# Operands of the up-projection made inside the out-projection, a reordered chain of head tiles, and the mixers' last stores moved behind their block

## The reference

```python
h = rms_norm(x, attn_norm_g); proj = h @ w_in            # 1024 -> 3600
q, k, v, z, xbc, dt_raw = split(proj)
attn_out = dilated_attention(q, k, v, q_norm_g, k_norm_g) # q and k normed per head; three patterns
ssm_out = ssd_mixer(z, xbc, dt_raw, ...)                  # conv, chunked scan, gate, rms_norm
x = x + concat(attn_out, ssm_out) @ w_out                 # 1536 -> 1024
x = x + conv_ffn(x, ffn_norm_g, w_up, ..., w_down)        # 1024 -> 5632, conv, gate, 2816 -> 1024
x = x + sigmoid(rms_norm(x, ple_norm_g) @ w_ple_gate) * (p @ w_ple_proj)
```

## Time and profile before

| What | us |
|---|---|
| Median of three runs | 3021.07 |
| Profiled execution | 3021.69 |
| Its span, first to last instruction | 3019.9 |
| PE busy | 2908.9 |
| DVE busy | 1999.8 |
| ACT busy | 1140.0 |
| POOL busy | 282.2 |

### The profile page before, as it was taken

How to read it: one execution, slowest core, us unless ns; L and a number is a source line. 1 busy time by engine, 2 the same in 40 slices (tenths; PEclk the granted TensorE clock), 3 DMA queues, 4 the chain that set the end, 5 groups by cost and what they waited for, 6 DMA issues and landing times. The chain is left out here.

```text
span 3019.9 us, 38703 instructions
## 1 busy us (share of the span) xinstructions
PE 2908.9 (96%) x14818; PEld 2296.6 (76%) x14818; DVE 1999.8 (66%) x2493; ACT 1140.0 (38%) x1735; POOL 282.2 (9%) x278
## 2 busy tenths in 40 slices
PE   8999999998989999899999999899999999999999
PEld 6788887875656566788778888788888788877887
DVE  7434555128566654545698899889998786776743
ACT  6321212112435353212254544544444444444321
POOL 0000000003433442000001000000000000000000
PEclk9999999998999999999999999999999999999999
DMA  4652222238585663643332244425543756453632
GB/s 150 201 164 75 63 82 68 63 112 202 169 213 146 193 173 103 205 143 115 141 110 79 98 147 156 179 90 192 193 153 105 257 200 227 146 158 114 195 115 67
DMA packets 260125, 435.04 MB, mean 144 GB/s; under 512 B 44049, under 2 KB 128529, under 8 KB 252913
## 3 DMA queue, kind: packets, MB, share of 16 engines
q1 hardware_dynamic: 255570, 408.32, 42.8%
q0 software_dynamic: 4384, 24.41, 2.3%
HBM read 312.18 MB, written 120.00 MB: 143 GB/s over the span
## 5 line engine op out<-in xcount | busy, mean ns | idle before, releaser
L103 PE MATMUL up_banks<-up_x_hi,up_w_hi 128*128 128x512 f32 x1232 | 483.5, 392 | 23.8 <-DVE up_x_lo L2734 8.2
L105 PE MATMUL up_banks<-up_x_hi,up_w_lo 128*128 128x512 f32 x1232 | 481.6, 391 | 0.0
L104 PE MATMUL up_banks<-up_x_lo,up_w_hi 128*128 128x512 f32 x1232 | 481.3, 391 | 0.0
L103 PE MATMUL inp_ps<-inp_h_hi,carry_q 128*128 128x512 f32 x896 | 352.9, 394 | 9.9 <-DVE inp_h_lo L200 9.8
L104 PE MATMUL inp_ps<-inp_h_lo,carry_q 128*128 128x512 f32 x896 | 349.7, 390 | 0.0
L105 PE MATMUL inp_ps<-inp_h_hi,carry_k_two 128*128 128x512 f32 x896 | 349.5, 390 | 0.0
L103 PEld LDWEIGHTS up_banks<-up_x_hi,up_w_hi 128*128 128x128 f32 x1232 | 232.4, 189 | 79.7 <-DVE up_w_lo L2667 16.1
L105 PEld LDWEIGHTS up_banks<-up_x_hi,up_w_lo 128*128 128x128 f32 x1232 | 232.3, 189 | 49.1
L104 PEld LDWEIGHTS up_banks<-up_x_lo,up_w_hi 128*128 128x128 f32 x1232 | 232.6, 189 | 47.8 <-issue 0.2
L2775 DVE SCALAR_TENSOR_TENSOR carry_rows<-carry_squares,up_conv_w,carry_rows 128x1024 f32<-128x1024 f32 x176 | 232.2, 1319 | 24.4 <-ACT carry_rows L2606 19.5
L103 PE MATMUL down_banks<-down_x_hi,down_w_hi 128*128 128x512 f32 x616 | 240.6, 391 | 7.1 <-DVE down_x_lo L2246 7.1
(11 more groups left out here) (384 smaller groups left out, 5332.6 us busy)
## 6 DMA issues: line engine op xcount, KB each, us to landing
carry_room<-in_w_up_dram SPq DMA_DIRECT2D x84, 512.0 KB, 4.4
act<-carry_rows SPq DMA_DIRECT2D x44, 512.0 KB, 2.8
carry_room<-cum_rows SPq DMA_DIRECT2D x16, 1024.0 KB, 6.8
carry_room<-x SPq DMA_DIRECT2D x7, 2048.0 KB, 9.8
carry_room<-in_w_in_dram SPq DMA_DIRECT2D x26, 512.0 KB, 6.0
xbc<-carry_room SPq DMA_DIRECT2D x12, 1024.0 KB, 5.7
carry_room<-xbc SPq DMA_DIRECT2D x16, 768.0 KB, 4.5
down_x<-act SPq DMA_DIRECT2D x12, 1024.0 KB, 7.4
```

Of the source, the lines that this page charges most:

```text
L103: pe.matmul(out, w_hi, x_hi, start=first, stop=False, skip_group_check=onto)
L104: pe.matmul(out, w_hi, x_lo, start=False, stop=False, skip_group_check=onto)
L105: return pe.matmul(out, w_lo, x_hi, start=False, stop=last, skip_group_check=onto)
```

## The change

Three parts.

1. **Head tiles.** DVE's split of the coming weights moves behind the low half of tile t-1, and ACT's high half of them behind the high half of t-1. SP's `spread_inverses` is cut in two: `fold_roots` now comes ahead of SP's wait for the split weights and the load of the next ones, the rest stays behind the load. `add_up(2)` in product 3 comes before k = 5 instead of k = 3, in products 4 and 5 before k = 4; from product 6 on it stays at 3.
2. **Mixers' end.** The last round's fold goes to a place of its own, and its inverse on DVE, its two stores and the store of `y_root` are issued by the out-projection's block: on SP ahead of `load(None)`, with the waits for all of them, on DVE ahead of k = 1.
3. **Up-projection's operands.** The high and low halves of A11, A12 and S1 and the difference S1 are made in the out-projection: 12 ACT and 16 DVE instructions, on DVE between the 16 of L1929 and `finish(NB - 1)`. The up-projection raises its semaphores by their counts instead.

```diff
-def column_tile(pe, out, w_hi, w_lo, h_hi, h_lo, mm_done, between=None):
+def column_tile(pe, out, w_hi, w_lo, h_hi, h_lo, mm_done, between=None, ahead=3):
-        if k == 3 and between:
+        if k == ahead and between:
...
-            def spread_inverses(t):
+            def fold_roots(t):
                 sp.wait_ge(ps_free, t + 1)
                 if t > 0:
                     sp.wait_ge(inverse_st, 16 * t)
                 for e in range(2):
                     sp.dma_start(fold[HD * e:HD * e + HD, :], roots[16 * e:P:32, :]).then_inc(folded, 16)
+
+            def spread_inverses(t):
                 sp.wait_ge(inv_done, t + 1)
...
                 else:
+                    if 2 <= t < QKT + 2:
+                        fold_roots(t - 2)
                     sp.wait_ge(wlo_done, t + 1)
                 sp.dma_start(w_raw[t % 2], w_tiles[(t + 2) * P:(t + 3) * P, :]).then_inc(w_in_s[t % 2], 16)
...
-                    split(t, 0, b) if t % 2 == 0 else split(t - 1, 0, b)      # ACT
                 if 0 < t <= QKT:
                     high(t - 1)
+                if t > 0:
+                    split(t, 0, b) if t % 2 == 0 else split(t - 1, 0, b)
...
                     evacuate(t, b, stage[b])                                  # DVE
-                    split(t - b, 0, b)
                 if 0 < t <= QKT:
...
                     low_part(t - 1)
+                if t > 0:
+                    split(t - b, 0, b)
...
-            product(3, 1, ps_free, lambda: add_up(2, 0))
+            product(3, 1, ps_free, lambda: add_up(2, 0), None, 5)
             for i in range(1, QKT // 2 - 1):
-                product(i * 2 + 2, 0, ps_free, lambda: add_up(i * 2 + 1, 1))
-                product(i * 2 + 3, 1, ps_free, lambda: add_up(i * 2 + 2, 0))
+                product(i * 2 + 2, 0, ps_free, lambda: add_up(i * 2 + 1, 1), None, 4)
+                product(i * 2 + 3, 1, ps_free, lambda: add_up(i * 2 + 2, 0), None, 4)
...
-            sp.dma_start(self.mix_t[r * P:(r + 1) * P, :], out).then_inc(self.o_st, 16)
+            if r < KVH - 1:
+                sp.dma_start(self.mix_t[r * P:(r + 1) * P, :], out).then_inc(self.o_st, 16)
...
+    def last_stores(self, sp):
+        sp.dma_start(self.mix_t[(KVH - 1) * P:KVH * P, :], self.out_last[:, :]).then_inc(self.o_st, 16)
+        self.store_inverse(sp, KVH - 1)
         sp.wait_ge(self.o_st, 16 * KVH)
         sp.wait_ge(self.inv_st, 16 * KVH)
...
+            mixer.store_root(sp)             # out_projection, SP
+            heads.last_stores(sp)
+            sp.wait_ge(mixer.root_st, 16)
             load(None)
...
+                    if first and k == 1:     # out_projection, DVE
+                        heads.invert(dve, KVH - 1)
...
+            for v, freed in ((A11, 2), (A12, 8), (S1, 4)):        # out_projection, ACT
+                act.wait_ge(k_done, NB * MIXT + freed)
+                for q in range(Q):
...
+                    act.activation(x_hi[:, v, q], at, ACT.Copy).then_inc(next_hi, 1)
...
+            dve.wait_ge(carry.normed, 2 * KD)                     # out_projection, DVE
+            dve.wait_ge(k_done, NB * MIXT + 4)
+            next_low(0, A11)
+            dve.wait_ge(k_done, NB * MIXT + 6)
+            for q in range(Q):
+                dve.tensor_tensor(x_raw[:, S1, q], carry.x_blk[1][:, q], carry.x_blk[0][:, q], ALU.subtract).then_inc(next_t1, 1)
+            dve.wait_ge(k_done, NB * MIXT + 10)
+            next_low(1, A12)
+            next_low(2, S1)
             finish(NB - 1)
...
             dve.wait_ge(carry.normed, 2 * KD)                     # up_projection, DVE
+            dve.sem_inc(x_lo_s, 3 * Q)
             weights(0)
-            tokens(0, 0)
             s1(0)
             weights(1)
-            tokens(0, 1)
-            for q in range(Q):
-                dve.tensor_tensor(x_raw[:, S1, q], x_blk[1][:, q], x_blk[0][:, q], ALU.subtract).then_inc(t1_s, 1)
             weights(2)
             s2(0)
-            tokens(0, 2)
```

More of the change, by code:

```diff
@@ L695, in turn, with product @@
                 last.then_inc(v_turned, 1)
-            def product(t, b, free, between=None, into=None):
+            def product(t, b, free, between=None, into=None, ahead=3):
                 pe.wait_ge(wlo_done, t + 1)
                 pe.wait_ge(free, t - 1)
-                column_tile(pe, ps[b] if into is None else ps[into], w_hi[:, b], w_lo[:, b], h_hi, h_lo, mm_done, between)
+                column_tile(pe, ps[b] if into is None else ps[into], w_hi[:, b], w_lo[:, b], h_hi, h_lo, mm_done, between, ahead)
             def time_steps():
@@ L1022, in sync_inverses, with store_inverse @@
     def sync_inverses(self, sp):
[L1023 removed]
+        for r in range(KVH - 1):
             yield self.at(2, r, 1.0) + self.OUT + 1.0
[L1025 to L1027 removed]
+            self.store_inverse(sp, r)
+    def store_inverse(self, sp, r):
+        sp.wait_ge(self.den_inv, r + 1)
+        sp.dma_start(self.den_rows[2 * r:2 * r + 2, :].rearrange("e (c s) -> (e c) s", s=32), self.fold(r)[:, 0, :]
+                     ).then_inc(self.inv_st, 16)
+    def last_stores(self, sp):
+        sp.dma_start(self.mix_t[(KVH - 1) * P:KVH * P, :], self.out_last[:, :]).then_inc(self.o_st, 16)
+        self.store_inverse(sp, KVH - 1)
         sp.wait_ge(self.o_st, 16 * KVH)
@@ L1178, in add, with fold, invert @@
             dve.tensor_tensor(den[0:2 * 32], bank[0:2 * 32, 1], den[0:2 * 32], ALU.add).then_inc(self.o_add, 1)
+    def fold(self, r):
+        return self.fold_last if r == KVH - 1 else self.den_fold
     def inverses(self, dve):
-        for r in range(KVH):
+        for r in range(KVH - 1):
             yield self.at(2, r, 1.0) + self.OUT
-            dve.wait_ge(self.den_in, 32 * (r + 1))
-            dve.tensor_tensor(self.den_fold[:, 0], self.den_fold[:, 0], self.den_fold[:, 1], ALU.add).then_inc(self.den_add, 1)
-            dve.wait_ge(self.den_add, r + 1)
-            dve.reciprocal(self.den_fold[:, 0], self.den_fold[:, 0]).then_inc(self.den_inv, 1)
+            self.invert(dve, r)
+    def invert(self, dve, r):
+        fold = self.fold(r)
+        dve.wait_ge(self.den_in, 32 * (r + 1))
+        dve.tensor_tensor(fold[:, 0], fold[:, 0], fold[:, 1], ALU.add).then_inc(self.den_add, 1)
+        dve.wait_ge(self.den_add, r + 1)
+        dve.reciprocal(fold[:, 0], fold[:, 0]).then_inc(self.den_inv, 1)
     def tensor(self, pe):
@@ L1770, in out_projection @@
     with Phase(nc, "outp") as ph:
+        Q = KD // 2
+        A11, S1, A12 = 0, 1, 3
+        with nc.sbuf_tensor("up_x_hi", [P, 7, Q, 512], F32R) as x_hi:
+            with nc.sbuf_tensor("up_x_raw", [P, 7, Q, 512], F32) as x_raw:
+                pass
+            with nc.sbuf_tensor("up_x_lo", [P, 7, Q, 512], F32R) as x_lo:
+                pass
+        carry.up_x = x_hi, x_raw, x_lo
         w_hi = ph.sb("w_hi", [P, MIXT, D], F32R)
@@ L2351, in up_projection @@
     with Phase(nc, "up") as ph:
-        x_hi = ph.sb("x_hi", [P, 7, Q, 512], F32R)
-        with nc.sbuf_tensor("up_x_raw", [P, 7, Q, 512], F32) as x_raw:
-            pass
-        x_lo = ph.sb("x_lo", [P, 7, Q, 512], F32R)
+        x_hi, x_raw, x_lo = carry.up_x
+        for part in ("hi", "lo"):
+            ph.sb(f"x_{part}_place", [P, 7, Q, 512])
         w_hi = ph.sb("w_hi", [P, RING, 512], F32R)
@@ L2614, in take_root @@
                 act.activation(rstd[n], banks[:, 3 if n == 2 else 7], ACT.Sqrt, bias=carry.eps[:, 0:1], scale=1.0 / D).then_inc(rooted, 1)
-            for n in range(3):
-                weights(n)
-                tokens(0, n)
-            for s in range(3, RING):
+            act.sem_inc(x_hi_s, 3 * Q)
+            for s in range(RING):
                 weights(s)
```

43 lines of the change are left out of this document (26 added, 17 removed).

## The result

The changed kernel takes 3008.9 us (median of 7 runs, 3006.48 to 3014.09), the kernel before 3025.6 us (median of 7, 3020.65 to 3029.64). The ratio is 0.9949, with a 95% interval of 0.9938 to 0.9960: faster by 0.4 to 0.6%, which is 12 to 19 us. The profiled pair differs by 15.2 us (3021.69 and 3006.48 us), where the prediction's sum was 15.0.

A forecast was written before the change was run, and what follows sets the result against it. The prediction took PE, busy 96% of the span, to bound the kernel. Its terms 3.1 + 6.5 + 5.4 = 15.0 us came off 3021.69 to give 3006.7, stated as 3006 us; range for 8 in 10, 3000 to 3013.

The forecast's parts named there:

- three terms: Whole kernel: gains of 3.1 us at the head tiles, 6.5 at the mixers' end and 5.4 at the up-projection.
- Head tiles, 3.1 us forecast: Head tiles: the chain decides add_up(5), 169.9 against 173.46, 3.6 us gained, less 0.5 for lost clock.
- N + 17.55: Head tiles: tile t+2's evacuation comes 17.55 us after N(t), the start of multiplying by tile t's inverse roots; unchanged.
- N(3): Head tiles: start of the multiplication by tile 3's inverse roots, put at 148.1 with 22.5 us per tile.
- N(0): Head tiles: start of the multiplication by tile 0's inverse roots, at 80.59, claimed to stay.
- its own refutation: Head tiles: the forecast is wrong if norm_rows lands more than 4.5 us after its issue.
- the rival with the load ahead of the roots: Head tiles: norm_rows waits behind SP's weight load, N(t+1) 2.4 us later per tile, 3013 us in all; chance 0.25.
- 3.4 + 8.1: Head tiles: norm_rows lands in 3.4 us and the broadcasts 8.1 us after their issue, within each tile's step.
- Mixers' end, 6.5 forecast: Mixers' end: the out-projection's block starts at 1206.5, 6.5 us earlier, with the path to PE's first matmul unchanged.
- a sign of being wrong: Out-projection: a wait at k = 4 would show the forecast wrong; ready at 1233, PE there at 1234.
- The "seven" us of slack: Out-projection, k = 4: one us of slack after the change, where there were seven before.
- Up-projection, 5.4 forecast: Up-projection's start: weights(3)'s low half starts at 1495.8 instead of 1501.16, 5.4 us gained; bounds 4.4 and 9.7.

The follow-up runs named there:

- heads_alone: The kernel before with only the head tiles' part of the change (edits in the in-projection); ratio 0.9996 (0.9986 to 1.0006).
- store_first: The changed kernel with SP issuing the small norm_rows store ahead of the next tile's 512 KB weight load; ratio 0.9957 (0.9942 to 0.9973).
- end_alone: The kernel before with only the mixers' end moved (last fold, its inversion, three last stores into the out-projection's block); ratio 0.9974 (0.9964 to 0.9984).
- split_early: The changed kernel with tile 3's weights split ahead of the multiplication by tile 0's roots on ACT and DVE; ratio 0.9948 (0.9931 to 0.9964).
- x1_after_load: The changed kernel with the store of x1's last 2 MB issued behind the up-projection's group 1 loads; ratio 0.9944 (0.9928 to 0.9960), median 3006.42 us.
- all_three: The changed kernel with the edits of store_first, split_early and x1_after_load together; ratio 0.9941 (0.9927 to 0.9956).
- operands_alone: The kernel before with only the up-projection's operands moved into the out-projection; ratio 0.9967 (0.9955 to 0.9980).
- load_last_split_early: load_last with tile 3's weights split early, as in split_early; ratio 0.9951 (0.9937 to 0.9964).
- load_last: The changed kernel with SP issuing the next tile's weight load only after the fold, the norm_rows store and the two broadcasts; one run, 3010.07 us.
- best: load_last_split_early with x1's last store behind the loads of group 1; ratio 0.9933 (0.9921 to 0.9946), median 3006.42 us.

## Why the prediction was right

*The total.* 15.0 us were forecast, 15.2 are between the profiled executions and 16.7 between the medians. Two of its three terms hold by their own rows, and the third was too large. By the distances of their own the terms are 1.3 to 2.0, 6.25 and 5.7 us, 13.3 to 14.0 in all. The rest of the 15.2 is made of stretches in which the traces show no effect of the change (0.8 ahead of the head tiles and 1.2 behind PE's first matmul, less 0.2 and 0.6). That the sum was met to 0.2 us is luck; that it was met within 2 us is not.

*Head tiles, 3.1 us forecast, 2.0 measured (1.3 in `heads_alone`).* Product 3's start at 90.0 behind 2.4 us of waiting came at 89.61 behind 2.60; `add_up(2)` without a wait, and `add_up(5)` at 169.9 came at 170.68 behind 1.78. The evacuation at N + 17.55 was at N + 17.6 to 17.9 from N(1) on. N(3) was put at 148.1 and came at 148.70 on a clock that ran 0.8 us ahead, so 1.4 us late: 0.4 in N(0), which "stays" by the prediction and did not, and the rest in the first steps, 23.3 and 22.8 us for 22.5. Ahead of N(0), the weight load is now issued at 68.67 us, 1.6 us before the roots' store, where it was issued at 61.25 and had landed. It is not the load's place in the queue alone, since with the store ahead of it (`store_first`) N(0) is no earlier. In the first step the roots' store took 6.5 us, and had taken 4.5 before, not the 3.4 that the prediction took for every tile. The later steps were 22.4.

Inside a step two terms were wrong in opposite directions. `norm_rows` took 5.4 us for 3.4, beyond the 4.5 that the prediction named as its own refutation; that is the mechanism of the rival with the load ahead of the roots, and `store_first` shows it. The broadcasts, issued later, took 2 us less than the row of before. The rival had added its 2.4 us to an unchanged 8.1, and so had the forecast with its 3.4 + 8.1: both held a time fixed that changed with the transfer's place. The rival's mechanism came, its price did not, and with it fail the 3013 us.

*Mixers' end, 6.5 forecast, 6.25 measured.* The block's start is 1.9 us behind the fold's issue, for the 1.6 that were put. The prediction gave the clock no gain here. In the pair it has 1.2 us, in most other traces 0.2 to 0.5 (see `end_alone`). Was k = 4 late? Not in this execution: the SSD's 2 MB were issued at 1214.92 and landed 12.6 us later, the gain column, which the row names, was issued at 1215.40 and landed 12.3 us later, DVE started at 1227.82, and k = 4 was ready at 1230.30.

```profile
1227.82 0.75 DVE L1933 SCALAR_TENSOR_TENSOR carry_room<-carry_room,outp_g_col,carry_sums 128x512 f32<-128x512 f32 x1 [4.52 <-DMA outp_g_col<-in_ssm_norm_g_dram]
...
1229.62 0.68 DVE L1912 TENSOR_TENSOR outp_m_lo<-carry_room,outp_m_hi 128x512 fp32r<-128x512 f32 x1
```

PE has 96 matmuls ahead of k = 4; the 16th started at 1212.25, and 81 starts of 0.227 us later k = 4 is due at 1230.6. The slack was 0.3 us, where one was forecast. Even that is two errors that cancel. `load(None)` was put at 1212.5 to 1213.5 and came at 1212.60 on a clock that ran 2.6 us ahead, so some 2 us late, and the SSD's load was put at 14.5 us and took 12.6. The prediction called the wait at k = 4 a sign of being wrong; it did appear in two other kernels with the same end, 1.38 us in `split_early` and 0.33 in `store_first`. The "seven" us of slack before were 2.7: k = 4 was ready at 1238.05 and started at 1240.70. A further microsecond gained at this block's start would have been waited for here.

*Up-projection, 5.4 forecast, 5.7 measured.* The 16 instructions ran from 1458.83 to 1468.55 (9.7 us forecast and measured), `finish(3)` waited for PE by 0.52 us (0.5 forecast), DVE waited 3.70 us before `weights(3)` (about 4). `x1_after_load` shows the cause by taking it away. One detail was wrong: PE waited also 1.90 us for the low half of a token operand at 1496.78, behind it in DVE's list.

## What to carry to other kernels

A wait of the bounding engine is worth only what the chain behind it can give: here PE's 5.70 us and 2.60 us could be taken away and came back as waits one and two tiles later, while the 1.1 to 1.5 us off the chain's step were kept to the end of the head tiles. Where several queues kept the DMA engines busy (a share of 0.8 here), reordering one queue moved waiting from one transfer to the next; a step is then to be summed over all transfers that the next one waits for, not over the one moved. Where a load that is waited for stood behind a large store that nobody waits for, changing the two paid 3.4 us for moving one line.

A difference in slow matmuls behind a wait, read from one pair of traces, is not yet an effect: it was 1.2 us in the pair here, and in further traces the 16th matmul came after 5.3 us behind the long wait, and after 6.3 us behind the short one.

## What the runs showed of the hardware

The clock behind a wait, by the eight small matmuls of a sum of squares: they took 1.09 to 1.10 us behind waits of 0.17 to 2.32 us, and 1.94 to 1.95 behind waits of 3.15 (`all_three`) to 5.84 us (`operands_alone`), which is the higher level (2.4 GHz) for the first and the lower (1.2 GHz) for the second. But eight fast matmuls do not say that the clock held behind them. The wait of 2.60 us before product 3 was followed, from about one microsecond behind it, by a lower clock: in the changed kernel the granted clock is 0.59 from 90 to 94 us and 0.99 in the 4 us behind, some 1.6 us of loss (4 times 0.41). The same came behind 2.04 us before `add_up(5)` of `load_last_split_early` (0.62 over the next 4 us), and behind 2.33 us before product 3 of `load_last` (0.59) the lower level was there at once. Behind 2.14 us (`load_last`, before `add_up(5)`), 2.17 (`split_early`), 2.30 (`all_three`) and 2.32 us (`best`) the granted clock stayed at 1.00 over the next 4 us. Ahead of the waits of 2.04, 2.33 and 2.60 us PE had been busy without a pause for 5 us or more at a granted clock of 1.00. So waits of 2.0 to 2.6 us went either way; on what that hangs the runs do not tell.

```profile
90.00:94.00 4.00, 4.00 (x12) 3.11 (x11) 0.00 (x0) 2.35 (x1) 0.53 (x1) 0.59 0.95 308
94.00:98.00 4.00, 4.00 (x19) 3.31 (x18) 0.00 (x0) 0.00 (x0) 0.00 (x0) 0.99 0.90 343
```

The wait of 2.04 us in `load_last_split_early`:

```profile
171.23 1.09 PE L696 MATMUL inp_ps<-inp_squares,carry_chunk_decay 128*32 128x512 f32 x8 [2.04 <-ACT inp_squares L493]
```

A stretch that no edit touches is not the same from one execution to the next: from DVE's last inversion of the norm to the fold at the mixers' end it was 1143.8, 1149.3 and 1148.6 us in the three traces whose work up to that fold is that of before (the kernel before, `end_alone`, `operands_alone`). That spread of 5.5 us is about as much as the two larger terms, and it is why each was read from a distance of its own.
